# Cached attention of the decode samples: one stream of loads, keys turned on VectorE, scores from 32x32 stationary tiles

## What is computed

```python
k_past = cache_k[page_table, :, l].reshape(DB, past, DIFF_HEADS, 2 * DIFF_DQK)   # 8 x 8192 x 4 heads x 128
v_past = cache_v[page_table, :, l].reshape(DB, past, DIFF_HEADS, DIFF_DV)        # 8 x 8192 x 4 heads x 128
s = jnp.concatenate([diff_scores(q, k_past), diff_scores(q, k_new)], axis=-1)    # two 64-wide halves per head
p = jax.nn.softmax(jnp.where(mask, s, -jnp.inf), axis=-1)
w = p[:, :, 0] - lam * p[:, :, 1]
o = einsum('bhqk,bkhv->bqhv', w[..., :p], v_past) + einsum(..., w[..., p:], v_new)
```

## Time and profile before

| | |
|---|---|
| median of 3 runs | 2482.78 us |
| profiled execution, span from the first to the last instruction | 2519.8 us (its own time outside the span is not given) |
| cache attention, first load issued to last output | 784.05 to 1622.6 us, 838 us |
| busy share of the span: PE, DVE, ACT, POOL | 82%, 50%, 43%, 16% |
| HBM read over the span | 531 MB, of which this stage 268 MB |

### The profile page before, as it was taken

How to read it: one execution, slowest core, us unless ns; L and a number is a source line. 1 busy time by engine, 2 the same in 40 slices (tenths; PEclk the granted TensorE clock), 3 DMA queues, 4 the chain that set the end, 5 groups by cost and what they waited for, 6 DMA issues and landing times. The chain is left out here.

```text
span 2519.8 us, 40027 instructions
## 1 busy us (share of the span) xinstructions
PE 2071.6 (82%) x14525; PEld 1517.6 (60%) x14525; DVE 1260.2 (50%) x1975; ACT 1084.1 (43%) x1919; POOL 397.7 (16%) x370
## 2 busy tenths in 40 slices
PE   7999988978886776867768677599729999999991
PEld 5777767755554554545545455335427888888881
DVE  4314404435664341433424234233358898988884
ACT  4313213313443432523325243332227878777760
POOL 0000000000002323233232322100031121222113
PEclk9999989955888998999989999899859999999996
DMA  4121232010005988898888989652029999999985
GB/s 168 47 80 42 70 130 105 3 36 1 1 1 230 359 318 327 289 352 316 320 321 288 354 298 334 228 199 74 34 89 366 400 405 402 405 406 401 405 334 224
DMA packets 106649, 577.16 MB, mean 229 GB/s; under 512 B 14592, under 2 KB 19840, under 8 KB 53520
## 3 DMA queue, kind: packets, MB, share of 16 engines
q0 software_dynamic: 44448, 293.89, 31.0%
q1 hardware_dynamic: 62064, 281.22, 28.8%
HBM read 531.26 MB, written 43.81 MB: 228 GB/s over the span
## 5 line engine op out<-in xcount | busy, mean ns | idle before, releaser
L1790 DVE TENSOR_TENSOR e_l<-first_w,e_h 128x1024 fp32r<-128x1024 f32 x256 | 294.8, 1219 | 11.0 <-ACT e_h L1787 10.8
L1185 PEld LDWEIGHTS ps<-ident,d_ring 128*128 128x128 f32 x2048 | 234.7, 147 | 106.9 <-issue 100.9
L1252 ACT COPY d_kT<-ps 128x512 f32<-128x512 f32 x256 | 149.9, 586 | 330.1 <-PE ps L1185 329.1
L1787 ACT CAST e_h<-first_w 128x1024 fp32r<-128x1024 f32 x256 | 250.2, 1049 | 84.0 <-POOLq L1859 42.4
L1185 PE MATMUL ps<-ident,d_ring 128*128 128x128 f32 x2048 | 265.6, 285 | 9.8 <-DMA d_ring<-in_cache_k,d_row 6.8
L1749 PE MATMUL ps<-e_h,e_xh 128*128 128x512 f32 x512 | 206.8, 404 | 3.8 <-DVE e_xl L1799 3.8
L1750 PE MATMUL ps<-e_l,e_xh 128*128 128x512 f32 x512 | 203.7, 398 | 0.0
L1751 PE MATMUL ps<-e_h,e_xl 128*128 128x512 f32 x512 | 203.7, 398 | 0.0
L1299 DVE COPY d_kT<-ps 128x512 f32<-128x512 f32 x256 | 172.4, 687 | 35.0 <-PE ps L1185 34.4
L1195 PE MATMUL ps<-d_kT,d_q 128*32 128x512 f32 x1024 | 135.4, 603 | 49.8 <-ACT d_kT L1252 48.7
L1303 DVE TENSOR_REDUCE d_top<-d_s 128x1 f32<-128x512 f32 x128 | 87.8, 686 | 172.6 <-ACT d_s L1256 159.0
(11 more groups left out here) (321 smaller groups left out, 3588.4 us busy)
## 6 DMA issues: line engine op xcount, KB each, us to landing
first_w<-in_w_down SPq DMA_DIRECT2D x32, 2048.0 KB, 19.4
first_w<-in_w_up SPq DMA_DIRECT2D x62, 1024.0 KB, 9.0
first_w<-in_w_gate SPq DMA_DIRECT2D x62, 1024.0 KB, 11.2
ys_d<-e_y SPq DMA_DIRECT2D x32, 512.0 KB, 9.9
w<-in_w_in SPq DMA_DIRECT2D x6, 2048.0 KB
ys_d<-cat SPq DMA_DIRECT2D x1, 8192.0 KB, 24.7
kT<-in_x_prompt SPq DMA_DIRECT2D x8, 512.0 KB, 4.5
m_wout<-in_w_out SPq DMA_DIRECT2D x2, 2048.0 KB, 10.6
```

Of the source, the lines that this page charges most:

```text
L1185: mm = pe.transpose(k.ps[:, h, r * P:(r + 1) * P], ring[:, g % RING, r, h * P:(h + 1) * P], ident)
L1252: act.copy(kT[:, g % 2, h, :], k.ps[:, h, :]).then_inc(s_kta, 1)
L1787: return act.copy(h13[:, :, kk, :], w13[:, :, kk, :])
L1790: return dve.tensor_tensor(l13[:, :, kk, :], w13[:, :, kk, :], h13[:, :, kk, :].bitcast(F32), ALU.subtract)
```

## The change

`sample_attention` is written again around a class `Past`, without hardware loops.

- **One stream.** All 256 loads stand in one list: step n loads the keys of group n (0 to 127, over all samples), and the values of group n - 20 (`LAG`). So there are 20 loads of keys, then keys and values by turns, then 20 loads of values. The ring has 4 slots in place of 8. A slot of keys is free when VectorE has turned it, a slot of values when TensorE has multiplied it.
- **Keys.** VectorE turns a whole load, 128 x 2048, in one instruction, square by square of 32x32, into `d_kB`. TensorE no longer turns keys, and `d_kT` and its copies are gone.
- **Scores.** After the turn the 128 dimensions of a head lie in four blocks of 32 (`d`), and each 32 partitions (`i`) hold another page. For four groups together (`t`), TensorE issues 64 matmuls of a 32x32 stationary tile and 512 columns: partitions 32i to 32i+32 go to PSUM bank i, head h to PSUM partitions 32h to 32h+32, and the four blocks d are summed. ScalarE copies four banks, 2048 scores, in one instruction; VectorE takes one maximum of 2048; ScalarE takes one exponential of 2048.
- **Order.** Every engine follows the same step number. In step n TensorE does, for n a multiple of 4, the scores of the four groups before n, then one turn of probabilities (group n - 19), then the values of group n - 20. VectorE turns the keys of group n, then, for n a multiple of 4, takes the maximum, then copies the turned probabilities. The softmax of a sample runs while the next one's keys come in.
- **Ahead of it.** The row numbers are made first, and GpSimd issues from them without a copy; three fills of zeros and 18 small copies that spread the queries come behind that on VectorE.

The core of the diff (new lines; what stood for them before is in the listing above):

```diff
+class Past:
+    RING = 4
+    LAG = 20
+    SLOTS = 5
+    UNITS = SAMPLES * GROUPS
+    LAST = UNITS + LAG
...
+        self.loads = [(c, n - c * self.LAG) for n in range(self.LAST) for c in range(2)
+                      if 0 <= n - c * self.LAG < self.UNITS]
...
+    def load(self, pool, x):
+        c, n = self.loads[x]
+        b, g = divmod(n, GROUPS)
+        if x >= self.RING:
+            before, m = self.loads[x - self.RING]
+            pool.wait_ge(self.s_pv if before else self.s_kb, m + 1)
+        pool.indirect_dma_start(out=self.ring[:, x % self.RING].rearrange("p r n -> p (r n)"), ...)
...
+    def scores(self, pe, t):
+        pe.wait_ge(self.s_kb, 4 * t + 4)
...
+        if t:
+            pe.wait_ge(self.s_sc, t)
+        keys = self.kB[:, t % 2].rearrange("p u (r h d t) -> p u r h d t", r=GROUP, h=HEADS, d=4)
+        for d in range(4):
+            for i in range(4):
+                for h in range(HEADS):
+                    part = slice(32 * i, 32 * i + 32)
+                    mm = pe.matmul(k.ps[32 * h:32 * h + 32, self.score_bank + i, :], self.q_now[part, b % 2, h, d, :],
+                                   keys[part, :, :, h, d, :], start=d == 0, stop=d == 3)
+        mm.then_inc(self.s_qk, 1)
...
+    def pe(self, pe, n):
+        if n % 4 == 0 and 4 <= n <= self.UNITS:
+            self.scores(pe, n // 4 - 1)
+        for b, what in self.small_of(n):
+            self.small(pe, b, what)
+        if n >= self.LAG:
+            self.values(pe, n - self.LAG)
...
+    def dve(self, dve, n):
+        k, (b, g) = self.k, divmod(n, GROUPS)
+        if n < self.UNITS:
+            keys = self.arrived(dve, 0, n)
+            if n >= 8:
+                dve.wait_ge(self.s_qk, n // 4 - 1)
+            dve.transpose(self.kB[:, n // 4 % 2, n % 4, :], keys.rearrange("p r n -> p (r n)")).then_inc(self.s_kb, 1)
+        if n % 4 == 0 and 4 <= n <= self.UNITS:
+            t = n // 4 - 1
+            dve.wait_ge(self.s_sc, t + 1)
+            top = dve.reduce_max(self.top[...], self.s[:, t % self.SLOTS].rearrange("p i n -> p (i n)"), axis=X)
...
+        for b, what in self.small_of(n):
...
+                dve.tensor_copy(self.pT[:, u % 2], bank.rearrange(...)[:, :, :, 0:8]).then_inc(self.s_smf, 1)
...
 def sample_attention(nc, k, io):
-    RING = 8
...
+                for x in range(len(past.loads)):
+                    past.load(pool, x)
...
+                for n in range(past.LAST):
+                    past.pe(pe, n)
```

More of the change, by code:

```diff
@@ L1097, in sample_attention @@
         sem = k.sem
[L1098 to L1107, removed]
@@ L1118, in sample_attention @@
[L1118 to L1123, removed]
@@ L1124, in sample_attention @@
[L1124 to L1127, removed]
+        past = Past(nc, k, io, ctx, (0, 4, 5))
+        table = past.s[:, 0].rearrange("p i n -> p (i n)")[:, 0:SAMPLES * PAGES].bitcast(I32).rearrange("p (b n) -> p b n", b=SAMPLES)
+        rows_f = past.s[:, 1].rearrange("p i n -> p (i n)")[:, 0:SAMPLES * GROUPS].rearrange("p (b n) -> p b n", b=SAMPLES)
@@ L1152, in _ @@
             def _(pool):
[L1153 to L1168, removed]
@@ L1270, in _ @@
+                for n in range(past.LAST):
+                    past.act(act, n)
             @block.vector
             def _(dve):
-                chain = Chain(dve, s_ch)
-                dve.memset(zeros[:], 0.0).then_inc(s_z, 1)
-                chain.link(dve.memset(q_pad[:], 0.0))
-                for c in range(2):
-                    chain.link(dve.tensor_copy(q_pad[64 * c:64 * c + 64, :, :, STEPS * c:STEPS * c + STEPS],
-                                               k.qTs[64 * c:64 * c + 64].rearrange("p h (b t) -> p b h t", t=STEPS)))
@@ L1331, in _ @@
-                chain.end(SAMPLES)
+                dve.tensor_copy(past.rows[:], rows_f).then_inc(past.s_rows, 1)
+                past.chain.link(dve.memset(past.q_new[:], 0.0))
+                past.chain.link(dve.memset(past.q_now[:], 0.0))
+                past.chain.link(dve.memset(past.q[:], 0.0))
+                for c in range(2):
+                    t = slice(STEPS * c, STEPS * c + STEPS)
+                    past.chain.link(dve.tensor_copy(past.q_new[64 * c:64 * c + 64, :, :, t],
+                                                    k.qTs[64 * c:64 * c + 64].rearrange("p h (b t) -> p b h t", t=STEPS)))
+                    for d in range(2 * c, 2 * c + 2):
+                        for i in range(4):
+                            ins = dve.tensor_copy(past.q[32 * i:32 * i + 32, :, :, d, t],
+                                                  k.qTs[32 * d:32 * d + 32].rearrange("p h (b t) -> p b h t", t=STEPS))
@@ L1332, in _ @@
+                past.chain.link(ins)
+                past.query(dve, 0)
+                for n in range(past.LAST):
+                    past.dve(dve, n)
                 dve.wait_ge(s_back, 16)
```

290 lines of the change are left out of this document (149 added, 141 removed).

## The result

The changed kernel takes 2501.82 us (median of 4 runs, 2497.39 to 2505.49), the kernel before 2482.70 beside it (2481.28 to 2486.34). The ratio is 1.0073, 95% interval 1.0056 to 1.0089: slower by 0.7%. The forecast was 2381, in a range of 2318 to 2490. The sign was wrong, and the time lies outside the range.

The account below looks back on a forecast made before the run. TensorE's order and its handovers with the copying engines were taken as the bound. The new stage summed 17.0 + 66 + 597 + 52 + 4 to 736 us, 102 off the median: 2381, range 2318 to 2490.

Parts of the forecast that it names:

- The base of the subtraction: Samples' cache attention stage: 838 us in the earlier profile, 736 forecast; 103 us less, scaled by 0.985 to 102.
- The standstill between samples: Ring of loads between samples in the kernel before: GpSimd waited 9.46 us for a slot of keys, rate 0 until 1110.
- The prices: Assumed times in us: VectorE's turn 2.3, ScalarE's copy 1.8, maximum 2.3, pT copy 0.3, values 1.5, scores 5.5.
- Rival (b): TensorE's scores: row groups of the 32x32 tiles run one behind another, scores 14.0 us, total 2628; chance 0.10.
- (c): VectorE's turn of keys takes two passes, 4.6 us, a round 24.4, total 2479, no change; chance 0.10.
- Rival (d): TensorE's instructions come late in a burst of scores: 10.5 us, total 2520; chance 0.13 with whatever lies between.
- The clock: TensorE's granted clock in the stage falls after pauses, to between 0.6 and 0.9, lengthening scores and values.
- rival (a): TensorE holds the upper clock and the ring covers the rest: rounds of 19.9 us, total 2322; chance 0.17.
- The round: Eight loads, four of keys and four of values, mid-stream: 22.1 us each, 27 rounds, 597 us.
- 19.9 + (v + s - 4.8): Round's length: 19.9 us for eight loads at full rate, plus values (v) and scores (s) beyond 4.8 where positive.
- The samples' ends: Eight ends of samples in the stream add 0.5 us each, 4 us.
- Start and end: First four keys turned 17.0 us, four rounds of keys alone 66, last 20 loads of values and output 52.

Follow-up runs that it names:

- the second profile: The kernel before, profiled again with nothing edited: span 2485.7 us; its runs 2486.05 us against 2483.22, ratio 1.0005.
- a_spread: Changed kernel with a group's scores spread over four steps, copy, maximum and exponentials later, values' lag 23 steps instead of 20: 2383.43 us, ratio 0.9592.
- a_quarter: Changed kernel with scores from only one of the four quarters of a head's 128 numbers (another output): 2406.36 us, ratio 0.9683.
- a_latemax: Changed kernel with VectorE's maximum one step later, behind the next turn of keys: 2423.17 us, ratio 0.9757.
- a_new6: Changed kernel with the scores of a sample's new tokens moved from its step 4 to its step 6: 2476.11 us, ratio 0.9970.

## Why the prediction was wrong, step by step

**The base of the subtraction.** The prediction took 103 us off a stage of 838 us and scaled by 0.985. It knew that the profiled execution was 37 us longer than the runs and spread that over the whole span. In fact the excess lay in this one stage (35.5 us over seven samples), which takes 799 in a usual execution. Against 799 the forecast of 736 was worth 63 us, not 103. The standstill between samples of the earlier trace rows goes with that excess: in the second profile the rate is 419 and 410 GB/s there. This is the first step that failed, and it costs 40 us.

**The prices.** Right: the turn 2.30 (2.3), the copy 1.87 (1.8), the maximum 2.29 (2.3), pT 0.27 (0.3), values 1.06 to 1.90 with a mean of 1.57 (1.5). Scores 5.9 us in the median (5.5), in a range of 4.8 to 7.2. But the values that count in the chain are those directly ahead of the scores, and they took 1.84 on average. Rival (b) wanted 14 and (c) 4.6 for the turn: both are excluded. Rival (d), late instructions, wanted 10.5: excluded as well. The Trainium skill's 10.6 times ("TensorE: Matmul & The Clock Gate", Part 3), by the estimate in the prediction 5.2 us at the upper clock, was bettered here: the shortest burst took 4.79 us at a mean granted clock of 0.93, and four of the pieces of a_spread, 1.15 us each at 1.00, make 4.6.

**The clock.** Forecast between 0.6 and 0.9, measured 0.75; right. No run held the scores in one piece at the upper clock. That it would have brought rival (a)'s rounds of 19.9 us is made unlikely by a_quarter: its scores took 2.0 us, less than the 3.6 that (a) counts on, and its rounds still 21.6. (The 676 us of (a) also keep the 66 us for keys alone, which go with scores of 5.5; with 3.6 they would be 59. Nothing here hangs on it.)

**The round.** 22.1 forecast, 24.2 measured; 20 rounds, 42 us. This is the second step that failed. The formula, 19.9 + (v + s - 4.8), gives 22.8 with the measured v = 1.84 and s = 5.9; so 0.7 is from prices and 1.4 from its form. Two things in the form failed. It let three other loads be in motion while the slot of keys waited for the maximum, but the values' slot waits behind the same scores, so that both holders of the ring were late in the same round; in the round shown this costs some 0.8 us. And its base of 19.9 is not reached: at a DMA share of 0.98 eight loads take 21.5 (a_spread). Either could make most of the 1.4, and no run divides it between them. That the place of the maximum was the lever is shown by a_latemax. The prediction had that wait in its chain and priced it too low.

**The samples' ends.** 0.5 us each forecast, 5.7 more than forecast for a round measured (27.8 against 22.1); seven, some 36 us. The prediction did not look at which step the new tokens' scores share, though its last sentence named the kind of thing: another wait that holds the slots of values. It is the third step that failed, and a_new6 shows it alone: 26 us for moving it.

**Start and end.** First four keys turned after 17.5 us (17.0): right. Four rounds of keys 70 (66). From the last scores to the last output 60 (52). Together 12 us.

The terms add up: 42 + 36 + 12 = 90, the difference between 826 and 736. And 63 - 90 = -27, of which some 10 us come back outside of the stage (1677 us in the profile of after, 1687 in the second one of before, 4.8 of them by an earlier first load). That leaves the 17 us between the two spans (2503.0 against 2485.7); the runs are 19 us apart.

**The range and the chances.** A slower kernel had been given 0.18, almost all for mechanisms that did not occur. What decided, two mis-sized terms, 12 us at the start and end, and a wrong base, was in none of the rivals; the forecast's own high end (24.1 a round, 2440) was computed from the same base.

## What to carry to other kernels

If the profiled execution is longer than the timed runs, find the stage that holds the excess, by a second profile or by a run with less of the stage, before anything is subtracted from it; scaling by the ratio puts it in the wrong place. In a ring, write down for every slot who frees it and what stands ahead of that on its engine: here one maximum, ahead of the instruction that frees a slot and itself waiting for another engine, cost 3% of the kernel, and one small operation in the wrong step 1%. Work that comes in one piece of 6 us may be worth cutting into pieces of a step's length if a ring of few slots waits behind it; here that gave 40 us together with the other moves of a_spread.

## What the runs showed of the hardware

- VectorE turned 128 x 2048 float32 in 32x32 squares in 2.30 us, as long as a maximum over the same elements (2.29).
- Sixteen float32 matmuls on all sixteen 32x32 tiles, 512 columns each, took 1.15 us at a granted clock of 1.00 (2.4 GHz) and 2.03 at 0.50 (1.2 GHz), in pieces of a_spread. They ran side by side in rows and columns at once: four matmuls on the quarters of the columns alone took 1.07.

```profile
888.18:889.33 1.15, 1.15 (x37) 0.31 (x34) 0.00 (x0) 0.00 (x0) 0.79 (x1) 1.00 1.05 442
...
1015.70:1017.73 2.03, 2.03 (x37) 0.37 (x34) 0.79 (x1) 1.39 (x2) 1.36 (x2) 0.50 0.55 194
```

- The same kernel was profiled once with steps of values of 2.31 us on TensorE and once with 1.95, 5 us a sample apart, with no change in the program; the timed runs fit the second.
- Transfers of 1 MB by indirect DMA ran at 389 GB/s beside VectorE's turns with a DMA share of 0.98, and at 411 with a share of 1.01 when the turns were cut to 64 columns; by one profile of each, somewhat under half of the difference (399 GB/s) came with the earlier freeing of the slot.
